# Moving the closing norm of a hybrid decoder trunk from token-major blocks to channel-major tiles

## The reference, cut to what matters

```
def rmsnorm(x, g):
    xf = x.astype(jnp.float32)
    y = xf * lax.rsqrt(jnp.mean(xf * xf, axis=-1, keepdims=True) + EPS)
    return (y * g.astype(jnp.float32)).astype(x.dtype)

def sq_relu_mlp(u, w_up, w_down):
    h = jax.nn.relu(jnp.einsum('btd,df->btf', u, w_up))
    return jnp.einsum('btf,fd->btd', h * h, w_down)
...
        x = x + sq_relu_mlp(rmsnorm(x, g_ffn[i]), w_up[i], w_down[i])
    return rmsnorm(x, g_final), ...
```

## Time and profile before

| what | value |
|---|---|
| median of 3 runs | 1607.14 us |
| lowest and highest of the runs | 1602.21 and 1893.83 us |
| span of the profiled execution, slowest core (core 2) | 1604.9 us |
| spans of the 8 cores | 1589.7 to 1604.9 us |
| own device time of the profiled execution | not among the runs shown |
| TensorE matmul busy | 1546.0 us, 96% |
| VectorE, ScalarE, GpSimd busy | 848.0, 567.6 and 114.1 us (53%, 35%, 7%) |

### The profile page before, as it was taken

How to read it: one execution, slowest core, us unless ns; L and a number is a source line. 1 busy time by engine, 2 the same in 40 slices (tenths; PEclk the granted TensorE clock), 3 DMA queues, 4 the chain that set the end, 5 groups by cost and what they waited for, 6 DMA issues and landing times.

```text
span 1604.9 us, 28273 instructions; the slowest of 8 cores (1589.7 to 1604.9 us)
## 1 busy us (share of the span) xinstructions
PE 1546.0 (96%) x10154; PEld 899.5 (56%) x10154; DVE 848.0 (53%) x1924; ACT 567.6 (35%) x1071; POOL 114.1 (7%) x245
## 2 busy tenths in 40 slices
PE   3899989999999999999999999999999999999997
PEld 3875545555556655555555555554555555555565
DVE  4756774655443444445676665775554444442335
ACT  4756444542112221222133224543643211223453
POOL 2002121110000000000000001121110000000000
PEclk9999999999999999999999999999999999999999
DMA  8968995676436506056000008896665452000112
GB/s 223 213 113 157 190 200 129 124 162 105 78 61 131 114 1 106 13 94 110 1 1 1 1 1 147 160 216 129 161 135 90 74 103 53 14 1 1 40 67 107
DMA packets 91860, 153.58 MB, mean 96 GB/s; under 512 B 4894, under 2 KB 42014, under 8 KB 91708
## 3 DMA queue, kind: packets, MB, share of 16 engines
q0 software_dynamic: 67568, 84.08, 34.1%
q1 hardware_dynamic: 24156, 67.70, 13.8%
HBM read 220.81 MB, written 14.42 MB: 147 GB/s over the span
## 4 chain that ended last, share of the span: by engine, by line
PE 85%; DMA 5%; DVE 4%; ACT 2%; issue 2%; POOL 0%; DVEq 0%; ACTq 0%; SPq 0%; POOLq 0%
PE PS L293 82%; DMA MEM<-cv 3%; DVE MEM L328 3%; PE PS L297 2%; ACT MEM L320 2%; DMA MEM<-gv 1%; PE PS L302 1%; DMA MEM<-x 1%; DVE MEM L332 1%; ACT MEM L309 1%; DVE MEM L340 0%; DVE MEM L346 0%; POOL MEM L355 0%; ACT MEM L344 0%; DVEq L1419 0%
## 5 line engine op out<-in xcount | busy, mean ns | idle before, releaser
L293 PE MATMUL PS<-MEM 128*128 128x416 bf16 (+6 forms) x8874 | 1462.0, 325 | 7.8 <-DVE MEM L346 3.0
L293 PEld LDWEIGHTS PS<-MEM 128*128 128x128 bf16 (+1 forms) x8874 | 827.7, 98 | 628.8 <-issue 34.9
L332 DVE TENSOR_TENSOR MEM<-PS,MEM 128x416 f32<-128x416 f32 (+6 forms) x558 | 312.6, 576 | 346.8 <-PE PS L293 278.5
L320 ACT ACTIVATE MEM<-PS 128x416 f32<-128x416 f32 (+5 forms) x469 | 238.8, 510 | 571.2 <-PE PS L293 559.9
L332 DVE TENSOR_TENSOR MEM<-MEM 128x416 bf16<-128x416 f32 (+3 forms) x282 | 161.3, 585 | 238.6 <-ACT MEM L320 228.5
L320 ACT ACTIVATE MEM<-MEM 128x416 bf16<-128x416 f32 (+9 forms) x299 | 185.5, 630 | 142.1 <-DVE MEM L332 111.7
L328 DVE SCALAR_TENSOR_TENSOR MEM<-MEM 128x416 bf16<-128x416 f32 (+7 forms) x322 | 177.0, 601 | 60.3 <-ACT MEM L320 50.4
L297 PE MATMUL PS<-MEM 128*128 128x128 bf16 (+6 forms) x1096 | 73.8, 265 | 26.2 <-DVE MEM L340 9.6
L305 DVE SCALAR_TENSOR_TENSOR MEM<-MEM 128x256 f32<-128x256 f32 x256 | 90.8, 420 | 4.1 <-DMA MEM<-qrows 4.1
L344 ACT COPY MEM<-PS 128x512 f32<-128x512 f32 (+3 forms) x73 | 39.2, 536 | 124.3 <-PE PS L293 113.4
L297 PEld LDWEIGHTS PS<-MEM 128*128 128x128 bf16 (+3 forms) x1096 | 51.9, 104 | 48.4 <-issue 47.4
(11 more groups left out here) (28 smaller groups left out, 137.4 us busy)
## 6 DMA issues: line engine op xcount, KB each, us to landing
MEM<-ck SPq DMA_DIRECT2D x64, 512.0 KB, 8.2
MEM<-cv POOLq DMA_DIRECT2D x64, 256.0 KB, 8.5
MEM<-w_down POOLq DMA_DIRECT2D x6, 2048.0 KB, 16.2
MEM<-x SPq DMA_DIRECT2D x16, 512.0 KB, 13.7
MEM<-w_kv POOLq DMA_DIRECT2D x4, 2048.0 KB, 16.6
MEM<-w_o POOLq DMA_DIRECT2D x4, 2048.0 KB, 22.1
MEM<-w_up POOLq DMA_DIRECT2D x32, 256.0 KB, 20.4
MEM<-qrows SPq DMA_DIRECT2D x32, 256.0 KB, 8.1
```

The source lines that it names most:

```text
L293: P.add(PE, "c", lambda e, o=out.ap, l=lhsT.ap, r=rhs.ap: e.matmul(out=o, lhsT=l, rhs=r, start=start, stop=stop), [lhsT, rhs], [out])
L320: P.add(ACT, "c", lambda e, o=out.ap, i=in_.ap: e.activation(out=o, in_=i, func=func, bias=bias, scale=sc), rd, [out])
L332: P.add(eng, "c", lambda e, o=out.ap, a=in0.ap, b=in1.ap: e.tensor_tensor(out=o, in0=a, in1=b, op=op), [in0, in1], [out])
```

## The change

The closing norm stays channel-major and is made per tile. The squares of a tile are made by ScalarE in pairs of chunks within the tile's last stB, right behind the residual additions (`summed`). The sums (`norm_p`, `norm_r`) and the scaling are entries of `fill`, taken one item later: norm_p, an empty entry, norm_r, and four entries that each scale two chunks (`stt` on VectorE) and store them. The rest stage takes an entry after every group (`pace`): those of tile 3. The last stage takes norm_p and norm_r of the 272 columns. Behind it come the sums of the last 128 columns (8 matmuls with a full block of ones, Ln, Exp), the scaling of the 272 columns and that of the 128. Nothing of it runs on GpSimd. The square of h in the last quarter moves from ScalarE to VectorE. y and ys leave the core as [channels, tokens] and are transposed on the host.

```
-    y_d = dout("y", [SEQ, D])
-    ys_d = dout("ys", [NS, D])
+    y_d = dout("y", [D, SEQ])
+    ys_d = dout("ys", [D, NS])
...
-                if q == 0 or (l == 1 and q == 3):
+                if q == 0:
                     act(h(fc, sl(0, n)), r(sl(0, n)), AF.Square)
                 else:
                     tt(h(fc, sl(0, n)), r(sl(0, n)), r(sl(0, n)), ALU.mult)
...
                 tt(X(ec, sl(c0 + a0, c0 + a1)), PSv(bk, 0, a1 - a0), X(ec, sl(c0 + a0, c0 + a1)), ALU.add)
+                if summed[0] is not None:
+                    summed[0](ec)
                 if mid is not None:
                     mid(ec)
...
-            if (c in (1, 4, 6) or l == 1 and c == 3 and len(fill) > 2) and not todo and fill:
+            if (c in (1, 4, 6) or pace or l == 1 and c == 3 and len(fill) > 2) and not todo and fill:
...
+        def store(a, b, out, c0, c1):
+            m = min(b, SEQ)
+            for o_d, u0, u1, o0 in ((y_d, a, m, 0), (ys_d, max(a, SEQ) - SEQ, b - SEQ, max(a, SEQ))):
+                if u1 > u0:
+                    w = out(sl(c0, c1), sl(max(o0 - a, 0), max(o0 - a, 0) + u1 - u0))
+                    dma(SP, DV(o_d.rearrange("(c p) t -> p c t", p=128)[:, c0:c1, u0:u1]), w, f"out{ctr[0] % 2}")
...
+            def sq(c):
+                if c % 2:
+                    act(SQ(sl(c - 1, c + 1)), X(sl(c - 1, c + 1), sl(a, b)), AF.Square)
+
+            def scale(cs):
+                for c in cs:
+                    stt(out(c), X(c, sl(a, b)), G(c, sl(R_FINAL, R_FINAL + 1)), RS(sl(0, n)), ALU.mult, ALU.mult)
+                for c in cs[::2]:
+                    store(a, b, out, c, c + 2)
+
+            return sq, lambda: norm_p(0, SQ, RS, n), lambda: norm_r(0, SQ, RS, n), scale, RS
+
+        def tile(ti):
+            sq, p, r, scale, _ = block(TILES[ti][0], TILES[ti][0] + TILES[ti][1], U3[ti])
+            return sq, [p, None, r] + [lambda c=c: scale((c, c + 1)) for c in range(0, NCH, 2)]
+
+        def rest():
+            t0, n = TILES[NT - 1][0], TILES[NT - 1][1]
+            sq, p, r, scale, _ = block(t0 + TAIL, t0 + n, T(U3[NT - 1].off, BF16, [NCH, n - TAIL]))
+            return sq, [p, None, None, r], lambda: scale(range(NCH))
+
+        def last():
...
+            def stat():
+                bk = nxt()
+                for c in range(NCH):
+                    mm(PSv(bk, 0, TAIL), ONESB(), SQ(c), c == 0, c == NCH - 1)
+                act(PSv(bk, 0, TAIL), PSv(bk, 0, TAIL), AF.Ln, scale=1.0 / D, bias=EPS)
+                act(RS(sl(0, TAIL)), PSv(bk, 0, TAIL), AF.Exp, scale=-0.5)
...
+        elif at and at[0] == "A" and at[1] >= 3 * NT:
+            if at[1] < 4 * NT - 1:
+                summed[0], its = f_tile(at[1] - 3 * NT)
+            else:
+                pace.append(1)
+                summed[0], its, r_scale = f_rest()
         elif at and at[0] == "T":
+            fill.extend(its)
+            summed[0], l_stat, l_scale = f_last()
+        elif at and at[0] == 3 and at[1] < NT - 1:
+            fill.extend(its)
+    assert not fill
+    l_stat()
+    r_scale()
+    l_scale()
```

More of the change, by code:

```diff
@@ L460, in build_program @@
     late = []
+    pace, summed = [], [None]
     def project(Wt, memn, dst, st, od, k, chan):
@@ L1332, in finish_phase @@
     def finish_phase():
[L1333 to L1339, removed]
-        ctr = [0]
[L1342 to L1349, removed]
+        OUT, RST = [], []
@@ new lines, in finish_phase @@
+        for i in range(2):
+            o = claim(f"final{i}").off
+            OUT.append(T(o, F32, [NCH, TW]))
+            RST.append(T(o + OUT[i].nbytes, F32, [TW]))
+        ctr = [0]
+        def store(a, b, out, c0, c1):
[4 more added lines that the diff above has]
+                    dma(SP, DV(o_d.rearrange("(c p) t -> p c t", p=128)[:, c0:c1, u0:u1]), w, f"out{ctr[0] % 2}")
@@ L1350, in final_block, with block @@
+        def block(a, b, SQ):
+            n = b - a
             k = ctr[0] % 2
             ctr[0] += 1
[L1352 to L1358, removed]
@@ L1359, in final_block @@
-            dma(SP, DV(ys_d if a >= SEQ else y_d[a:b, :]), st(p=(0, m)), f"stg{k}")
-        return final_block
+            RS = RST[k]
+            out = OUT[k] if n == TW else T(OUT[k].off, F32, [NCH, n])
+            def sq(c):
[6 more added lines that the diff above has]
+                    store(a, b, out, c, c + 2)
@@ new lines, in last @@
+        def last():
+            t0 = TILES[NT - 1][0]
+            SQ = T(U3[NT - 1].off + NCH * (TILES[NT - 1][1] - TAIL) * 2, BF16, [NCH, TAIL])
+            sq, _, _, scale, RS = block(t0, t0 + TAIL, SQ)
+            def stat():
[4 more added lines that the diff above has]
+                act(RS(sl(0, TAIL)), PSv(bk, 0, TAIL), AF.Exp, scale=-0.5)
+            return sq, stat, lambda: scale(range(NCH))
@@ L1363, in build_program @@
+        return tile, rest, last
     prelude()
@@ L1377, in build_program @@
     conv_phase()
-    done = [0]
     fill = []
[L1381 to L1387, removed]
     for at in attn_phase(1, fill):
         if at == (2, NT - 1):
[L1390 to L1394, removed]
-        elif at and at[0] == "T":
[L1396 to L1402, removed]
+            f_tile, f_rest, f_last = finish_phase()
+        elif at and at[0] == "A" and at[1] >= 3 * NT:
[4 more added lines that the diff above has]
+                summed[0], its, r_scale = f_rest()
+        elif at and at[0] == "T":
+            fill.extend(its)
[6 more added lines that the diff above has]
+    l_scale()
     sems = {e: es.enter_context(nc.semaphore(f"s_{e}")) for e in (PE, ACT, DVE, POOL)}
@@ L1514 @@
     g = lambda k: [np.asarray(r[k], dtype=np.float32) for r in rs]
-    y_prompt = np.stack(g("y"), 0)
-    y_sample = np.concatenate(g("ys"), 0).reshape(NCORES * NS, 1, D)
+    y_prompt = np.ascontiguousarray(np.stack(g("y"), 0).transpose(0, 2, 1))
+    y_sample = np.ascontiguousarray(np.stack(g("ys"), 0).transpose(0, 2, 1)).reshape(NCORES * NS, 1, D)
     new_pool_prompt = np.stack(g("npp"), 0)[None]
```

## The result

| | before | changed kernel |
|---|---|---|
| median of 7 runs | 1607.14 us | 1609.09 us |
| lowest | 1602.21 us | 1606.42 us |
| ratio to before | | 1.0038, 95% interval 1.0022 to 1.0054 |
| profiled execution, slowest core | 1604.9 us | 1607.1 us (device time 1608.7) |

The ratio leaves out runs in a slower state of the chip (three of 7 before, one of 7 after); the other runs have medians of 1603.2 and 1608.9 us.

What follows compares the result with a forecast made beforehand. TensorE's instruction time or new waits bound it until the last matmul, forecast at 1587.8 us; the tail of 10.6 gave 1598.4, 6.5 below the 1604.9 span, hence 1600.6 us from the 1607.14 median; range 1593 to 1608.

Steps and rivals of the forecast that it cites:

- Tile 3: two new waits: Rest and last stage: TensorE waits 1.0 us for tile 3's norm_p and 3.3 us for norm_p of the 272 columns.
- Waits inside the tiles: Tiles 0 to 2: norm_p's squares need 3.3 us, norm_p comes at 4.2 us, so TensorE waits nothing.
- Gain on TensorE up to tile 3: Until the end of tile 3's stB: 7.8 us of transposes removed, 2.7 us of norm matmuls added, 5.1 us gained.
- Cover of norm_p in tiles 0 to 2: In the next stA: norm_p's squares are ready 0.9 us before norm_p comes.
- rival (b): Tiles 0 to 2: VectorE falls behind, norm_p waits some 1 us per tile, 3 us back, 1603.6 us; chance 0.13.
- Waits: TensorE waits 1.0 us at the head of the rest stage and 3.3 us in the last stage.
- Clock: Behind the last stage's wait of 3.3 us the granted clock falls, costing 1.6 us; nothing charged for the 1.0 us wait.
- Tail: Behind the last MLP matmul: 10.6 us, as long as before, bound by DMA engines with 7.5 us of stores.
- Rival (c): The ys stores' 64-byte packets cost 0.2 us each instead of 0.03, 10.8 us more, 1611.4 us; chance 0.10.
- Sum: Whole span: last matmul at 1587.8 us plus tail 10.6 gives 1598.4 us, 6.5 us less than 1604.9.

Runs made afterwards that it cites:

- e1_chan: Changed kernel with a store channel (semaphore) of its own for each pair of chunks; ratio 0.9945 to the kernel before, first closing-norm matmul to span end 96.2 us.
- e7_warm: Changed kernel with a store channel per pair of chunks, plus 22 unread matmuls ahead of norm_p in the last stage; ratio 0.9951 to the kernel before.

## Why the prediction was wrong

The step that failed is in "Tile 3: two new waits": "VectorE now has behind the addition of group 3 ... eight scalings of 416 columns and four additions, in order: 8 x 0.574 + 4 x 0.39 = 6.2 us". The times of the instructions were right. In e1_chan the same row of work runs from 1576.74 to the end of the last addition at 1582.73, 6.0 us. But the line was costed without the waits between its members. Three of the eight scalings wait 2.33 us each for the landing of the store before them, so that norm_p's squares come 7.2 us later than in e1_chan. One scaling of tile 2, which stands in tile 3's stB, waits 1.22 us, so that tile 3's squares come 1.3 us later; the step "Waits inside the tiles" left that out in the same way. I listed the stores of a block, and priced their packets, but not what waits behind a store on the side of the buffer's writer. The code that does it (`chan_count` at the time of adding) is in the kernel before as well, and the change gives all stores of y and ys two channels.

The rest, by the steps:

- **Gain on TensorE up to tile 3.** 5.1 us forecast, 5.1 measured. Cover of norm_p in tiles 0 to 2: no wait, so rival (b) fell.
- **Waits.** 1.0 and 3.3 us forecast, from the place of norm_p in the list to its last squares. Counted so, and not by the idle time alone, since norm_p's first six matmuls run within, e1_chan has 1.2 (1571.43 to 1572.62) and 3.3 us (1580.30 to 1583.62). The mechanism forecast is there in its full size. With the shared channel the same two are 2.5 and 10.5 us. What came on top is the other mechanism.
- **Clock.** 1.6 us charged, 1.6 measured by e7_warm. By the earlier trace rows a wait of 1.99 us could lower the clock; the prediction charged nothing at the head of the rest stage because it had that wait at 1.0 us. At 2.0 us it can: the rest stage took 9.10 us on core 0 and 7.46 on core 4 of the same execution, with waits of 1.97 and 2.04 us ahead of it. What decides it stays open. The two cores with 7.46 have the shortest closing stretches (104.5 and 104.9 us), the six others 106.5 to 107.6.
- **Tail.** 10.6 us forecast from the last MLP matmul, 10.4 measured from there. The size is right partly by luck. The DMA engines need 5.7 us and not 7.5. VectorE (5.2 forecast, 5.5 measured, which the prediction's own slope of 0.42 and 0.27 a scaling would have given) and SyncE, whose twelve issues come 0.48 us apart and not 0.37, set it side by side. Rival (c), the dear short packet, fell: the change is slower by another mechanism.
- **Sum.** Without the self-wait the sum stands: 6.5 us forecast, and e1_chan's closing stretch is 6.3 us shorter than that of the kernel before. With it 10.5 us come back, so it comes out 4.2 us slower. The ratio of 1.0038 is 6 us, and its interval is 3.5 to 8.7 us, which holds the 4.2.

The range, 1593 to 1608, missed the time by 1 us, because no rival was about a wait of VectorE on the stores.

## What to carry to other kernels

Where dependencies are tracked by a count on a shared semaphore, a wait for an old transfer is a wait for all that was issued on it since. When a step alternates compute and stores on one buffer, read for each writer which count it waits for, and either give each part in flight its own semaphore or issue the computes before the stores. Cost a run of instructions by who releases each of them, not by the sum of their lengths: here the name of one semaphore was worth 10.5 us, against the 5.1 that the removed transposes had gained. And where whole-kernel times scatter by 15 us between cores, compare from a common instruction near the change.

## What the runs showed that I had not expected

- Packets of 64 bytes to DRAM are cheap (0.010 us each, against 0.049 at 1 KB): the tail's stores, a third of whose packets have 64 bytes, fit a line through packets of 1 and 4 KB (5.7 us against 5.8).
- The same wait of 2.0 us of TensorE lowered the granted clock on one core (0.81 over the 9 us behind it) and not on another of the same execution.
- Where TensorE waits and the clock falls, matmuls whose result nobody reads can be faster than none: 22 of them, in a wait of 2.65 us, gave 1.6 us.
